# Attention of a two-block model: the first 512 score columns of the first map are issued alone

## The reference

```
q = qb.reshape(b, nblk, Q_BLOCK, H_DIFF, 2, DH)          # Q_BLOCK 128, H_DIFF 4, DH 64
s = einsum('bqhmd,bkhmd->bhmqk', qblk, k) * ATTN_SCALE
p = softmax(s, axis=-1)
a = p[:, :, 0] - lam * p[:, :, 1]
o = einsum('bhqk,bkhv->bqhv', a, v)
```

## Time and profile before

| | |
|---|---|
| median of 3 runs | 2892.82 us (2890.85 to 2893.32) |
| the profiled execution | 2892.7 us, span 2890.9 us |
| TensorE (PE) busy | 2820.3 us, 98% of the span |
| VectorE busy | 1432.4 us, 50% |
| ScalarE busy | 913.5 us, 32% |
| POOL busy | 627.4 us, 22% |
| granted TensorE clock, mean | 0.997 of full speed |
| attention's scores (L1813, L1816) | from 419.8 to 611.5 us of the span |

### The profile page before, as it was taken

How to read it: one execution, slowest core, us unless ns; L and a number is a source line. 1 busy time by engine, 2 the same in 40 slices (tenths; PEclk the granted TensorE clock), 3 DMA queues, 4 the chain that set the end, 5 groups by cost and what they waited for, 6 DMA issues and landing times.

```text
span 2890.9 us, 34606 instructions
## 1 busy us (share of the span) xinstructions
PE 2820.3 (98%) x14290; PEld 2338.5 (81%) x14290; DVE 1432.4 (50%) x1518; ACT 913.5 (32%) x1087; POOL 627.4 (22%) x319
## 2 busy tenths in 40 slices
PE   7999999999999999999999999999999999999997
PEld 4878777887788888788888888888777888888886
DVE  6478128877422226545555665656765213131236
ACT  4332217763211113444442222222333112121122
POOL 0111115104222224222221111111142222212222
PEclk9999999999999999999999999999999999999999
DMA  7211440023111112111111111111031111111113
GB/s 225 73 29 39 150 147 1 1 74 95 51 45 51 47 49 84 55 44 44 51 55 37 37 30 37 37 37 37 23 85 54 47 49 44 52 51 51 44 54 114
DMA packets 276884, 168.52 MB, mean 58 GB/s; under 512 B 5632, under 2 KB 270208, under 8 KB 276352
## 3 DMA queue, kind: packets, MB, share of 16 engines
q1 hardware_dynamic: 275296, 162.88, 19.2%
q10 hardware_dynamic: 1440, 3.51, 0.3%
HBM read 162.17 MB, written 4.19 MB: 58 GB/s over the span
## 4 chain that ended last, share of the span: by engine, by line
PE 60%; issue 27%; POOL 5%; DVE 4%; ACT 2%; DVEq 1%; SPq 0%; DMA 0%; POOLq 0%; ACTq 0%
PE PS L1500 16%; PE PS L1502 16%; PE PS L1501 16%; POOL Wlo L404 5%; PE PS L1948 3%; ACT exp L689 1%; DVE acol L1177 1%; PE PS L1676 1%; PE PS L1597 1%; PE PS L1953 1%; PE PS L1813 1%; PE PS L1982 1%; PE PS L1936 0%; PE PS L1685 0%; PE PS L1984 0%
## 5 line engine op out<-in xcount | busy, mean ns | idle before, releaser
L404 POOL TENSOR_TENSOR Wlo<-Wraw,Whi 128x1024 fp32r<-128x1024 f32 x237 | 564.5, 2382 | 1992.2 <-ACT Whi L487 1992.2
L1500 PE MATMUL PS<-Bh,Whi 128*128 128x512 f32 x2176 | 858.6, 395 | 3.5 <-POOL Wlo L404 1.3
L1502 PE MATMUL PS<-Bh,Wlo 128*128 128x512 f32 x2176 | 848.1, 390 | 0.0
L1501 PE MATMUL PS<-Bl,Whi 128*128 128x512 f32 x2176 | 847.5, 389 | 0.0
L487 ACT ACTIVATE Whi<-Wraw 128x1024 fp32r<-128x1024 f32 x237 | 247.2, 1043 | 767.4 <-PE PS L1502 765.1
L1500 PEld LDWEIGHTS PS<-Bh,Whi 128*128 128x128 f32 x2176 | 409.1, 188 | 93.2 <-DVE Bl L942 4.9
L1502 PEld LDWEIGHTS PS<-Bh,Wlo 128*128 128x128 f32 x2176 | 408.7, 188 | 86.3
L1501 PEld LDWEIGHTS PS<-Bl,Whi 128*128 128x128 f32 x2176 | 409.1, 188 | 82.9 <-issue 1.0
L1500 PE MATMUL PS<-Hh,Whi 128*128 128x512 f32 x1120 | 443.9, 396 | 4.9 <-issue 1.7
L1502 PE MATMUL PS<-Hh,Wlo 128*128 128x512 f32 x1120 | 436.2, 389 | 0.0
L1501 PE MATMUL PS<-Hl,Whi 128*128 128x512 f32 x1056 | 411.2, 389 | 0.0
(11 more groups left out here) (329 smaller groups left out, 3083.9 us busy)
## 6 DMA issues: line engine op xcount, KB each, us to landing
Wraw<-in_w_in SPq DMA_DIRECT2D x64, 512.0 KB, 4.0
Wraw<-in_w_down SPq DMA_DIRECT2D x38, 512.0 KB, 3.7
adaV<-in_ada_w SPq DMA_DIRECT2D x16, 1024.0 KB, 5.2
Wraw<-in_odd_w_in SPq DMA_DIRECT2D x32, 512.0 KB, 4.1
Wraw<-in_w_up SPq DMA_DIRECT2D x32, 512.0 KB, 4.1
Wraw<-in_even_w_in SPq DMA_DIRECT2D x24, 512.0 KB, 3.8
adaW<-in_ada_w SPq DMA_DIRECT2D x8, 1024.0 KB, 11.3
Wraw<-in_even_w_out SPq DMA_DIRECT2D x14, 512.0 KB, 3.8
```

The source lines that it names most:

```text
L404: pool.tensor_tensor(Wlo[:, slot, 0:tiles, :], Wraw[:, slot, 0:tiles, :], Whi[:, slot, 0:tiles, :].bitcast(F32), ALU.subtract).then_inc(lo ...
L1500: mm(out, Whi[:, u % 2, k, :], hi[:, k, c], start=(k == 0), stop=False)
L1501: mm(out, Whi[:, u % 2, k, :], lo[:, k, c], start=False, stop=False)
L1502: return mm(out, Wlo[:, u % 2, k, :], hi[:, k, c], start=False, stop=(k == KT - 1))
```

## The change

In `scores(b)` map 0's group of bank 0 (columns 0 to 511, all its terms) is issued first, alone. TensorE waits ahead of it for the first exponential of the block before (`exp_ready` 2b - 1), and behind it for the second (2b). Then come three groups: map 1's 256 with map 0's second 512; map 1's first 512 with map 0's last 256 (into bank 2); map 1's second 512 without partner. The wait for `shared_read` stands ahead of map 0's first matmul into bank 2 as before, which is now in the second of these groups, behind map 1's first matmul of it. The number of matmuls and the number of increments of each semaphore are the same. In `shifts(b)` the maximum of bank 0 comes first; then that of map 1's 256 columns, which raises `shared_read`; then map 0's other two.

```diff
         def shifts(b):
             s = b % 3
+            dve.wait_ge(sem("s0_psum"), 3 * b + 1)
+            dve.reduce_max(acol[:, s, 0:1], bank(0), AX.X)
             dve.wait_ge(sem("s1_psum"), 3 * b + 1)
             if b == 0:
                 dve.wait_ge(sem("s0_psum"), 3)
             dve.reduce_max(acol[:, s, 3:4], PS[:, S1:S1 + 256], AX.X).then_inc(sem("shared_read"), 1)
-            for i in range(3):
+            for i in range(1, 3):
                 dve.wait_ge(sem("s0_psum"), 3 * b + i + 1)
                 dve.reduce_max(acol[:, s, i:i + 1], bank(i, 512 if i < 2 else 256), AX.X)
...
+            end = len(terms) - 1
+
+            def one(n, k1, w1):
+                q, k = terms[n]
+                return mm(PS[:, S1 + k1:S1 + k1 + w1], q[64:128], k[64:128, k1:k1 + w1], start=(n == 0), stop=(n == end))
+
+            def zero(n, k0, w0):
+                q, k = terms[n]
+                return mm(PS[:, S0 + k0:S0 + k0 + w0], q[0:64], k[0:64, k0:k0 + w0], start=(n == 0), stop=(n == end))
+
+            if b:
+                pe.wait_ge(sem("exp_ready"), 2 * b - 1)
+            for n in range(len(terms)):
+                last = zero(n, 0, 512)
+            last.then_inc(sem("s0_psum"), 1)
             if b:
                 pe.wait_ge(sem("exp_ready"), 2 * b)
-            end = len(terms) - 1
-            for i, (k1, w1, k0, w0) in enumerate(((0, 256, 0, 512), (256, 512, 512, 512), (768, 512, 1024, 256))):
-                for n, (q, k) in enumerate(terms):
-                    one = mm(PS[:, S1 + k1:S1 + k1 + w1], q[64:128], k[64:128, k1:k1 + w1], start=(n == 0), stop=(n == end))
-                    if i == 2 and n == 0:
+            for i, (k1, w1, k0, w0) in enumerate(((0, 256, 512, 512), (256, 512, 1024, 256), (768, 512, None, None))):
+                for n in range(len(terms)):
+                    last1 = one(n, k1, w1)
+                    if i == 1 and n == 0:
                         pe.wait_ge(sem("shared_read" if b else "s1_psum"), b + 1)
-                    zero = mm(PS[:, S0 + k0:S0 + k0 + w0], q[0:64], k[0:64, k0:k0 + w0], start=(n == 0), stop=(n == end))
-                one.then_inc(sem("s1_psum"), 1)
-                zero.then_inc(sem("s0_psum"), 1)
+                    if i < 2:
+                        last0 = zero(n, k0, w0)
+                last1.then_inc(sem("s1_psum"), 1)
+                if i < 2:
+                    last0.then_inc(sem("s0_psum"), 1)
```

## The result

The changed kernel takes 2923.89 us in the median (2921.8 to 2924.05), against 2892.82 before: ratio 1.0107, 95% interval 1.0093 to 1.0121, so 31 us slower. The forecast was 2923.4. The profiled execution spans 2920.0 us.

The account below looks back on a forecast made before the run. Bound: TensorE, 98% busy; in attention, the exponentials-scores-maxima loop at 5.91 us. Early blocks 2.3, block 4 1.17, 27 periods 27.7, end -0.44: +30.7 on 2892.7 gives 2923.4 us; range 2909 to 2933.

Parts of the forecast that it names:

- Step 1: Start of scores: waiting only for the first exponential gains TensorE's idle 0.43 us a block and no more.
- Step 2: Map 0's three lone matmuls have no partner; VectorE's maximum of bank 0 starts 1.0 us after the first, nothing hiding it.
- block 0: First plain-fp32 block: waits for no maximum, but its second-map passes start 0.97 us late, costing 0.9 us.
- rival B: Kernel gets faster: needs a period under about 5.75 us, but TensorE's work with lone matmuls is 6.18; 3%.
- Step 3: VectorE's 512-wide maximum goes first: no VectorE time lost, but `shared_read` comes 0.60 us later, 2.02 after the first lone matmul.
- Step 4: TensorE's `shared_read` wait moves forward, more matmuls queue behind it: transposes 3.44 us after the first matmul, against 1.93.
- Rival A: At the `shared_read` wait only map 0's half is held, map 1's runs on: period 6.0, 2896 us, no change; 8%.
- Step 5: Steady attention blocks: 3.44 + 3.55 = 6.99 us a block against a mean of 5.964; 27 periods add 27.7 us.
- The exponentials hold nobody: ScalarE: the second exponential ends at 6.3 us, before the next block's first matmul; neither holds TensorE any more.
- ScalarE's wait for the first shift: Sign in the profile: ACT waits longer for VectorE's first shift, about 2.5 us against 1.41.
- The stretches of VectorE that some periods lose fall into its 0.97 of slack: Steady blocks: VectorE's lost time (mean period 5.964, quiet 5.91) is absorbed by its 0.97 us of slack.
- Blocks 2 and 3: Early plain-fp32 blocks: an earlier start shortens the idle 2.49 us between them; together +0.5 us, between 0 and 1.8.

Follow-up runs that it names:

- e6_second_exp: The changed kernel, but the lone first group waits for the second exponential of the block before, as before the change; 2928.59 us, ratio 1.0125.
- e4_both: Kernel before with bank 0's group early, map 1's 256 columns signalled at once, bank 2's group last, old order of maxima; 2890.0 us, ratio 0.9993.
- e1_old_maxima: The changed kernel with VectorE's maxima in the old order, map 1's 256 columns first; 2915.26 us, ratio 1.0080.
- e3_wait_late: The changed kernel, but map 0's bank 2 group and its `shared_read` wait go with map 1's last group; 2906.25 us, ratio 1.0046.
- e8_after_pool_waits: The changed kernel plus two waits on POOL: keys' subtraction and large splits of blocks 8 to 16 start after a combine; 2919.67 us, ratio 1.0094.

## Why the prediction was right, and where it was not

*Step 1 (start).* Right: the group starts 3.47 after the transposes, directly behind the output, and `e6_second_exp` shows that in the steady loop the earlier wait buys nothing.

*Step 2 (alone).* The time to the maximum, 1.00, was right; "three that run alone have no partner" was wrong. Map 1's first matmul is issued behind all three, and starts at 541.27, 0.01 after the first of them. As long as the exponential's wait is already met, a matmul of the other row half starts past those ahead of it in the stream. The error cost the sum nothing because TensorE then waits for `shared_read` whatever it did before. It made block 0 wrong (no cost in place of 0.9: it waits for no maximum, and its halves run side by side), and it made rival B wrong: TensorE's work is not 6.18 with a lone group, as the 5.75 of `e4_both` shows.

*Step 3 (order of the maxima).* Right in the change, 2.02. `e1_old_maxima` adds what I had not seen: taken back, it gains 0.14 and not 0.60, because the signal of map 1's first group comes late too.

*Step 4 (the wait).* Right, and the largest term: `e3_wait_late` moves that wait with its group, and nothing else, and takes the period from 6.91 to 6.21. The latency was 0.06 in place of 0.12. Rival A, the halves run on by themselves, is out: the second map 1 matmul of its group starts at 543.34, together with the waiting one, after standing still since the first at 541.84. The halves pass each other where nothing waits, and not past an unmet wait.

*Step 5 (period).* 6.99 against 6.90; 0.08 of the difference is that I took the end of the last output matmul (3.55) where the next start is free at the pace (3.47).

*The other engines.* The exponentials hold nobody, as worked out, and VectorE idles 0.87 ahead of its first maximum. ScalarE's wait for the first shift was forecast to grow to about 2.5 and is 1.7 (47.8/28): another 0.55 (15.4/28) it now waits earlier, for TensorE's output. "The stretches of VectorE that some periods lose fall into its 0.97 of slack" was the step that failed: in five periods VectorE's small operation ahead of the combine, which meets a subtraction of POOL's, took up to 1.68 in place of 0.22; 1.46 more is beyond the slack, and each period lost 0.5. With POOL's waits that goes (`e8_after_pool_waits`): the median is 4.2 us less, where 2.5 were expected, and the two profiled executions, 2921.8 and 2919.27, are 2.5 apart; what the median has beyond that is not accounted for. This error (+2.5) and that of the period (-2.4) cancel.

*Blocks 2 and 3.* +1.41 against +0.5, inside the bound of 1.8. Here too it was POOL, in rows of the change's timelines:

```profile
440.96 1.25 POOL L437 CAST kh<-kT 128x1280 fp32r<-128x1280 f32 x1
```

```profile
441.12 2.43 DVE L1197 SCALAR_TENSOR_TENSOR early<-early,acol,early 128x1280 f32<-128x1280 f32 x1
443.48 0.68 DVE L1172 TENSOR_REDUCE acol<-PS 128x1 f32<-128x512 f32 x1
```

The combine took 2.43, where the kernel before has 1.59 in that block, and block 3's first maximum started as it ended; TensorE then waited 0.80 for `shared_read`. After a combine of 1.59 it would have waited about 0.7 less, by my estimate (map 1's 256 columns are over at 442.51 + 0.81 = 443.32, and the maximum that frees the bank takes 0.41), most of the 0.91 by which this term missed. Block 0's 0.9 too much makes up for it. The landing within half a microsecond of the median is thus in part luck: four errors, each of 0.9 to 2.5 us, cancel in pairs. The loop, its place and its period to 0.09 are not.

## What to carry to other kernels

When a matmul waits for another engine's read of a shared bank, count what stands behind it in the stream: the engine's other row half is blocked with it, so such a matmul belongs as late as its result allows, and the read that frees it as early as its data allow. A group's signal comes only when every matmul ahead of it in the stream has ended, in the other half too, so put the signalled group ahead of what need not be waited for. Before a period is shortened or lengthened, look at which operations of VectorE and POOL on the SBUF will meet at the new period.

## What the runs showed of the hardware that was not expected

- Matmuls of the two row halves start out of their order in the stream: the fourth issued started 0.01 after the first (541.27 against 541.26), 0.57 ahead of the third (541.84). Their signals do not overtake: in `e1_old_maxima` a group over at 563.66 was answered by VectorE at 564.41 only. The ends of matmuls are modelled, so that delay is as exact as they are.
- A VectorE operation on two SBUF tiles that starts 0.08 after POOL's 2.91 takes 4.17 in place of 1.55; the one-column operation ahead of it up to 1.68 in place of 0.22. A copy on POOL with one input does it too (1.25 long: combines of 2.43 and 2.45). A one-input reciprocal on VectorE beside POOL's 2.37 kept its 0.17.
- The granted clock stayed at 1.00 with a gap of 0.43 us in every period of 6.9.
